# Third matrices and output projections: both halves of the activation in one pass over a whole bank

## The reference, cut to what matters

```
def swiglu(x, w_gate, w_up, w_down):
    return (jax.nn.silu(x @ w_gate) * (x @ w_up)) @ w_down     # w_down: 2816 x 1024

# first model, two layers: x += 0.5*ffn1(norm(x)); x += merged(attention) @ w_out; x += 0.5*ffn2(norm(x))
# second model:
        x = x + g_a * y_l                                      # y_l ends in a product with the output matrix
        x = x + g_m * sq_relu_mlp(modulate(rms_norm_2(x, norm_mlp_g[i]), sh_m, sc_m), mlp_w1[i], mlp_w2[i])
```

## Time and profile before

| | us |
|---|---|
| median of 3 runs | 2549.56 (2544.74 to 2553.31) |
| profiled execution | 2535.18 |
| its span, first to last instruction | 2533.3 |
| TensorE busy in the span | 2472.7 |
| VectorE busy | 1618.0 |
| ScalarE busy | 1191.0 |
| mean granted clock of TensorE | 0.987 |

### The profile page before, as it was taken

The page is one execution under the profiler, slowest core; times in us unless marked ns, Lnnn a source line. Parts: engine busy times, 40 slices in busy tenths (PEclk is TensorE's granted clock), DMA queues, the critical chain, the costliest instruction groups (busy, mean ns, idle before and its releaser), DMA issues.

```text
span 2533.3 us, 42329 instructions
## 1 busy us (share of the span) xinstructions
PE 2472.7 (98%) x18041; PEld 2309.1 (91%) x18041; DVE 1618.0 (64%) x2450; ACT 1191.0 (47%) x1960; POOL 332.4 (13%) x369
## 2 busy tenths in 40 slices
PE   8999999999999899999999999999999999999998
PEld 7999989999999899899999667888888999999998
DVE  4787576778987865767775875542443654556753
ACT  5444566544444355655454553531332534345643
POOL 1321000332022010022331000100001011001000
PEclk9999999999999999999999999999999999999999
DMA  7677544567776756347785120322322433334552
GB/s 252 208 234 211 154 138 134 181 219 241 254 233 216 237 141 196 109 142 251 264 285 165 51 79 17 98 96 89 100 99 85 127 104 113 100 100 152 172 193 100
DMA packets 386385, 401.65 MB, mean 159 GB/s; under 512 B 44695, under 2 KB 370611, under 8 KB 385940
## 3 DMA queue, kind: packets, MB, share of 16 engines
q1 hardware_dynamic: 383448, 391.19, 49.3%
q10 hardware_dynamic: 2748, 7.76, 0.8%
HBM read 394.72 MB, written 4.19 MB: 157 GB/s over the span
## 4 chain that ended last, share of the span: by engine, by line
PE 76%; DVE 15%; ACT 4%; DMA 2%; issue 2%; POOL 1%; ACTq 0%; DVEq 0%; POOLq 0%
PE bank L676 22%; PE bank L677 21%; PE bank L678 21%; DVE rounded L2419 7%; PE bank L684 4%; DVE plain L2404 3%; ACT rounded L1642 2%; DMA plain<-in_ffn_w_down 2%; PE bank L1565 2%; PE bank L689 1%; POOL plain L3497 1%; PE bank L1090 1%; DVE plain L2547 1%; PE bank L1120 1%; PE bank L779 0%
## 5 line engine op out<-in xcount | busy, mean ns | idle before, releaser
L676 PE MATMUL bank<-rounded 128*128 128x256 f32 (+1 forms) x3704 | 1116.6, 301 | 10.0 <-DVE rounded L2419 7.0
L677 PE MATMUL bank<-rounded 128*128 128x256 f32 (+1 forms) x3704 | 1099.4, 297 | 0.0
L678 PE MATMUL bank<-rounded 128*128 128x256 f32 (+1 forms) x3704 | 1099.2, 297 | 0.0
L2419 DVE TENSOR_TENSOR rounded<-plain,rounded 128x1024 fp32r<-128x1024 f32 (+1 forms) x630 | 738.3, 1219 | 459.0 <-ACT rounded L1642 459.0
L1642 ACT ACTIVATE rounded<-plain 128x1024 fp32r<-128x1024 f32 (+1 forms) x630 | 616.0, 1032 | 301.7 <-PE bank L678 186.3
L676 PEld LDWEIGHTS bank<-rounded 128*128 128x128 f32 x3704 | 714.3, 193 | 44.3 <-DVE rounded L2419 9.0
L677 PEld LDWEIGHTS bank<-rounded 128*128 128x128 f32 x3704 | 714.8, 193 | 16.0
L678 PEld LDWEIGHTS bank<-rounded 128*128 128x128 f32 x3704 | 714.2, 193 | 16.4
L676 PE MATMUL bank<-rounded,rounded 128*128 128x256 f32 (+2 forms) x1472 | 452.3, 307 | 17.3 <-DVE plain L2615 10.0
L678 PE MATMUL bank<-rounded,rounded 128*128 128x256 f32 (+2 forms) x1472 | 449.4, 305 | 0.0
L677 PE MATMUL bank<-rounded,rounded 128*128 128x256 f32 (+2 forms) x1472 | 448.7, 305 | 0.0
(11 more groups left out here) (310 smaller groups left out, 1992.2 us busy)
## 6 DMA issues: line engine op xcount, KB each, us to landing
plain<-in_mlp_w SPq DMA_DIRECT2D x64, 1024.0 KB, 5.3
plain<-in_ada_w SPq DMA_DIRECT2D x48, 1024.0 KB, 5.5
plain<-in_ffn_w_gate SPq DMA_DIRECT2D x44, 1024.0 KB, 6.1
plain<-in_ffn_w_up SPq DMA_DIRECT2D x44, 1024.0 KB, 6.0
plain<-in_ffn_w_down SPq DMA_DIRECT2D x32, 1024.0 KB, 5.3
plain<-in_w_in SPq DMA_DIRECT2D x32, 1024.0 KB, 5.4
plain<-in_od_w_in SPq DMA_DIRECT2D x32, 1024.0 KB, 5.7
plain<-in_ffn_w_down SPq DMA_DIRECT2D x16, 768.0 KB, 5.1
```

The costliest lines, as they stand in the source:

```text
L676: pe.matmul(dst, a[0], b[0], start=first and i == 0, stop=False)
L677: pe.matmul(dst, a[0], b[1], start=False, stop=False)
L678: ins = pe.matmul(dst, a[1], b[0], start=False, stop=last and i == n - 1)
L2419: dve.tensor_tensor(low, raw, top, SUB).then_inc(*done(("lo", m, half)))
```

## The change

In 7 of the 8 output groups (o = 0 to 6) of the six kinds of product named above, `apart` takes the place of `product`. It passes the top and the low activations as one moving operand of 512 columns, two pieces of 256 at a distance, under the top weights into the whole bank; then the top activations under the low weights into columns 0 to 255. So columns 0 to 255 hold top by top and low by top, and columns 256 to 511 hold top by low. VectorE adds both parts to the residual, the second one after it has waited for its own first addition. The bank is free and the group done with the second. Group 7 stays as it was. `p0` stays too, since it has 512 columns of tokens, and so does the even mixer.

```
@@ -678,6 +678,20 @@
+    def apart(b, pairs, first=True, last=True):
+
+
+        n = len(pairs)
+        for i, (a, (h, l)) in enumerate(pairs):
+            both = bass.AP(h.tensor, h.offset, [h.ap[0], [l.offset - h.offset, 2], *h.ap[1:]])
+            pe.matmul(b[:, :], a[0], both, start=first and i == 0, stop=False)
+            ins = pe.matmul(b[:, 0:256], a[1], h, start=False, stop=last and i == n - 1)
+        return ins
+
+    def sums(apart_, b):
+
+        return (lambda *a: apart(b, *a)) if apart_ else (lambda *a: product(b[:, 0:256], *a))
@@ -849,8 +863,8 @@
-                    ins = product(bs[j][:, 0:256], [(part(m, k - k0, j * 128), (f.hr[:, k, :], f.lr[:, k, :]))],
-                                  k == 0, k == 21)
+                    ins = sums(2 * blk + j < 7, bs[j])([(part(m, k - k0, j * 128), (f.hr[:, k, :], f.lr[:, k, :]))],
+                                                       k == 0, k == 21)
@@ -2490,6 +2507,20 @@
+    def second(b, o, by, keys):
+
+        for x in new(L.last()):
+            dve.wait_ge(*x)
+        dve.scalar_tensor_tensor(X[:, o, 0:256], b[:, 256:512], by, X[:, o, 0:256], MUL, ADD).then_inc(*done(*keys))
@@ -2612,8 +2643,11 @@
+                    keys = [(s, "x", o), ("free", s, "d", o)]
                     dve.scalar_tensor_tensor(X[:, o, 0:256], M.bank(s, "d", o)[:, 0:256], 0.5, X[:, o, 0:256], MUL,
-                                             ADD).then_inc(*done((s, "x", o), ("free", s, "d", o)))
+                                             ADD).then_inc(*done(*([] if o < 7 else keys)))
+                    if o < 7:
+                        second(M.bank(s, "d", o), o, 0.5, keys)
```

More of the change, by code:

```diff
@@ L1171, in mixer @@
                         keys = [("unit", m)] if j else []
-                        ins = product(bs[j][:, 0:256], [(part(m, k, j * 128), (b_.Mr[:, k, :], b_.Ml[:, k, :]))], k == 0, k == 7)
+                        ins = apart(bs[j], [(part(m, k, j * 128), (b_.Mr[:, k, :], b_.Ml[:, k, :]))], k == 0, k == 7)
                         if k == 7:
@@ L1177, in mixer @@
                     keys = [("unit", m)] if j else []
-                    product(bs[j][:, 0:256], [(part(m, k, j * 128), (b_.Mr[:, k, :], b_.Ml[:, k, :])) for k in range(8)]
+                    sums(2 * blk + j < 7, bs[j])([(part(m, k, j * 128), (b_.Mr[:, k, :], b_.Ml[:, k, :])) for k in range(8)]
                             ).then_inc(*done((s, "wo", 2 * blk + j), *keys))
@@ L1480, in mlp @@
                                 pe.wait_ge(*x)
-                            ins = product(bs[j][:, 0:n], [(part(m, k - k0, j * 128), (b_.hr[:, k, :], b_.lr[:, k, :]))],
-                                          k == 0, k == b_.part - 1)
+                            pairs = [(part(m, k - k0, j * 128), (b_.hr[:, k, :], b_.lr[:, k, :]))]
+                            if l and 2 * blk + j < 7:
+                                ins = apart(bs[j], pairs, k == 0, k == b_.part - 1)
+                            else:
+                                ins = product(bs[j][:, 0:n], pairs, k == 0, k == b_.part - 1)
                         keys = [("unit", m)] if j else []
@@ L1577, in outer @@
                 pe.wait_ge(*x)
-            return product(b[:, 0:256], [(part(m, k % 8, j * 128), (b_.Yr[:, k, :], b_.Yl[:, k, :]))], k == 0, k == 15)
+            return sums(2 * blk + j < 7, b)([(part(m, k % 8, j * 128), (b_.Yr[:, k, :], b_.Yl[:, k, :]))], k == 0, k == 15)
         bs = [[bank(s, "wo", j) for j in range(2)], None, None, None]
@@ L2491, in residual_part, with residual_two @@
                                  MUL, ADD).then_inc(*done((s, "x", o, q), ("free", *name)))
+    def second(b, o, by, keys):
+        for x in new(L.last()):
+            dve.wait_ge(*x)
+        dve.scalar_tensor_tensor(X[:, o, 0:256], b[:, 256:512], by, X[:, o, 0:256], MUL, ADD).then_inc(*done(*keys))
+    def residual_two(s, key, name, o, l, which, *out):
+        for x in new(at(*key)):
+            dve.wait_ge(*x)
+        b, by = M.bank(*name), M.MODS[l][:, 16 + 24 * which + o, 0:1]
+        dve.scalar_tensor_tensor(X[:, o, 0:256], b[:, 0:256], by, X[:, o, 0:256], MUL, ADD).then_inc(*done())
+        second(b, o, by, [out, ("free", *name)])
     def residual(s, key, name, o, l, which, seqs, *out):
@@ L2981, in mixer @@
                     dve.wait_ge(*x)
+                keys = [(s, "x", o), ("free", s, "wo", o)]
                 dve.tensor_tensor(X[:, o, 0:256], M.bank(s, "wo", o)[:, 0:256], X[:, o, 0:256], ADD).then_inc(
-                    *done((s, "x", o), ("free", s, "wo", o)))
+                    *done(*([] if o < 7 else keys)))
+                if o < 7:
+                    second(M.bank(s, "wo", o), o, 1.0, keys)
                 if o:
@@ L3380, in odd @@
                         o = 2 * blk + j
[L3381 removed]
+                        if o < 7:
+                            residual_two(s, (s, "wo", o, 8), (s, "wo", o), o, 1, 0, s, "x", o)
+                        else:
+                            residual(s, (s, "wo", o, 8), (s, "wo", o), o, 1, 0, 1, s, "x", o)
                         b1 = M.mlp[1]
```

6 lines of the change are left out of this document (4 added, 2 removed).

## The result

| | before | after |
|---|---|---|
| median of 13 runs, us | 2547.83 (2541.14 to 2553.31) | 2552.97 (2549.83 to 2569.32) |
| profiled execution, us | 2535.18 | 2553.40 |
| mean granted clock in it | 0.987 | 0.984 |

What follows compares the result with a forecast made beforehand. The prediction took TensorE, with 76% of the chain of waits, as the main bound and VectorE, with 15%, as the bound around the splits. Eight stretch terms summed to +8.9 us: 2549.6 + 8.9 = 2558.5 us, range 2546 to 2570.

Steps and rivals of the forecast that it cites:

- m0: Projection, up to TensorE's wait at 499.39: VectorE's chain holds the path, second additions lengthen its loops; +3.2 us.
- b0: Third matrix, up to TensorE's wait at 700.80: pairs of groups add 0.45, 0.92, 0.68 and 0.92; +2.9 us.
- a0: Third matrix: VectorE's chain up to the last pair +2.0, lower clock after a longer TensorE wait +1.6; +3.6 us.
- a1: Third matrix: VectorE's chain up to the last pair +2.0, low clock's stretch falling into the wait -1.0; +1.0 us.
- b1: Third matrix: TensorE never idle, loads almost as slow; -1.0 us counted of 154 triples' 1.8.
- p1: Last matrix: TensorE never idle, splits ready well ahead, so all 224 triples count; -2.7 us.
- The triple: Two matmuls, one of 512 columns, replace three of 256: 12 ns saved each, 12.8 us for all 1064 (8.8 to 15.9).
- the rival that saves nothing: The 512-column pass costs its columns and a second start, so triples save nothing or little; 2564 us, chance 0.06.
- The second addition: On VectorE, starts 0.45 us after the first; 0.46 us more per group, 26.6 us at most, some 13 on the path.
- Cold starts: Rival: longer stops in first products of b0, a1 and b1 bring the lower clock; 5.5 us more, 2564, chance 0.14.
- Half-absorbed additions: Rival: half of the 12.8 us of lengthening sinks in VectorE's gaps or pace-setting loads; +2.5 us, 2552, gaps' chance 0.20.
- Hidden additions: Rival: VectorE hides the additions, only the triples count; -12.8 us, 2537 (2534 to 2541), chance 0.12.

Runs made afterwards that it cites:

- C1: The change itself, first profile; 2553.40 us in that execution, ratio 1.0034 to the kernel before.
- C2: The change executed once more for its trace, nothing altered; 2562.18 us.
- S: The whole change, with top and low activations side by side in memory, so no jump in the operand; ratio 1.0027 to the kernel before.
- one-piece kernel: The change with the wide matmul's operand as 512 columns in one piece, adding up wrong products; 2547.85 us in its only run.
- V: VectorE's part alone: the kernel before plus 56 second additions of the same columns times zero, each waiting for the first; ratio 1.0057.
- P: TensorE's part alone: the change without its second additions, so top by low is left out; ratio 1.0000 to the kernel before.
- N: V with each second instruction not waiting for the first, writing to the bank's unused half; ratio 1.0027 to the kernel before.

## Why the prediction came out right, step by step

Own share means: the average of C1, C2, S and the one-piece kernel less the average of the profiles that are the kernel before in that stretch. In `o` and `p1` it is C1 and C2 alone, since the other two have no jump, and in `m0` and `m1` a profile with a low clock is left out and named.

| stretch | forecast | own share | |
|---|---|---|---|
| `m0` | +3.2 | +2.84 (3.1 with S's low clock) | mechanism right, one link too many |
| `m1` | +2.7 | +2.57; 4.13 with a low clock | right |
| `b0` | +2.9 | +2.7 | right, but unchanged programs spread over 2.8 |
| `a0` | +3.6 | +1.3 | chain 1.7 for 2.0, clock wrong |
| `a1` | +1.0 | +1.3 | right by two errors |
| `b1` | -1.0 | +0.3 | wrong; unchanged programs spread over 0.6 |
| `o` | -0.8 | -0.3 | triple mis-sized |
| `p1` | -2.7 | -1.3 | triple mis-sized |
| sum | +8.9 | +9.4 to +10 | measured +8.7 (4.6 to 13), 5.1 by the medians |

One part of the change's cost falls behind these stretches and stands in no row. The first 28 us of `m0` and of `m1` are each 0.3 us longer in the change (C1, C2, S and one piece), and the first 7 us of `e` 0.2. V has 0.3 and 0.15 there, P nothing, and each repeats within 0.02 us; in the table above they lie in the rows of the attentions and of `e`, where a low clock's 1.5 to 8 us hide them. The 0.3 is what the forecast had for group 7's addition and weighting in `a0` and `a1`, and it is right; for the 0.2 behind `b1` it had nothing. With these 0.8 us the sum is +10.2 to +10.8, still inside the interval.

**The triple** is the term that was mis-sized: 12 ns taken, 5.6 to 5.9 measured, below the lower end of the range (8.3). It came from `p0`'s contiguous 512 columns. The prediction named the jump as unknown, gave it no price above the tile's, and so cut its own range too short; the jump's 4 ns is what it lacked, and the rest is that the wide step without a jump is 234 and not 230, less 2 ns that the narrow step gives back (118.6 for 120.8). The prediction's last sentence named this sign, a step "well off 230 ns", and 238 is that. In `p1` it is the whole miss. For the triples alone the truth lay between the forecast and the rival that saves nothing.

**The second addition** was right to the hundredth (0.45 us behind the first, 0.92 a loop), and so was its place. In `m0` the four pairs of groups came out at 0.54, 0.92, 0.92 and 0.45; the forecast had 0.53, 0.92, 0.92 and 0.92. Group 7 has no second addition, and its weighting is only as late as group 6's makes it. The forecast counted a link that isn't there: its term for the last pair fails by 0.47, less the 0.1 it took off.

**The stop for a weighting** in `b0`'s first product was to be 2.7 us. It is 2.08 in C2, 0.63 in C1, where a low clock at 471 us had held TensorE back, but the end of the stretch is the same in both. The 2.5 us forecast in `b1` were 2.07. In `a1` none of note came: TensorE waits there 1.25 us for a split.

**`a0` and `a1`.** The chain up to the last pair has an own share of 1.7 us in both, near the forecast 2.0. The clock's +1.6 in `a0` rested on one execution in which the clock had stayed up; the kernel before pays this too, and the own share of the last pair is -0.4, in `a1` as well (forecast -1.0). The sum was saved by errors of opposite sign: `a0` was 2.3 too high (2.0 with the 0.3 us behind it), and `b1`, `o` and `p1` together were 3.2 too low. That the forecast came within 0.2 us of the measurement is luck; that `m0`, `m1` and `b0` carry most of it is not.

**`b0`.** The size came out (the forecast's four terms add up to 2.97, of which it took 2.9), but not by the steps that the forecast summed. In C1 TensorE stops before the last pair of groups for a split, and the low clock follows:

```profile
676.10 0.79 PE L687 MATMUL bank<-rounded,rounded 128*128 128x512 f32 x1 [2.22 <-DVE rounded L2436]
...
676.00:679.00 3.00, 2.90 (x9) 2.51 (x10) 2.97 (x5) 0.71 (x1) 0.00 (x0) 0.50 1.00 367
```

A stop of this size and a low clock behind it stand there in all four profiles with the whole of the change, and in none of the ten without it, P and V included; V and N have the additions, and +2.5 and +2.6, without it. So here there is a cold start that comes with both halves together: an early TensorE and a late VectorE. What it adds at the end of the stretch (0.9 us between V and the change) is within what the loads move there, and stays open.

**`b1`.** The forecast let seven second additions cost nothing, for want of weightings behind them, and gave the triples 1.0. V and N, with the additions alone, gave +0.6 and +0.8, but one unchanged program gave +0.6 too, so what the additions cost there is not clear of the spread. In the first trace of before the closest split of `b1`'s third matrix is ready 0.17 us ahead of its use, and TensorE never stops. In V it stops 0.36 us for that split, in C1 0.77 us, and 0.69 us for another:

```profile
1330.06 0.51 PE L687 MATMUL bank<-rounded,rounded 128*128 128x512 f32 x1 [0.77 <-DVE rounded L2436]
...
1347.94 0.50 PE L687 MATMUL bank<-rounded,rounded 128*128 128x512 f32 x1 [0.69 <-DVE rounded L2436]
```

An unchanged program stops 0.36 us for that split as well. So the margin of 0.17 us is what the forecast's "0.2 to 1.5 us ahead" had and didn't price, and how much of the loss is the additions' and how much the loads' stays open.

**The rivals.** Cold starts came in part, and not all where the forecast put them: in `b0`'s third matrix, ahead of its last pair of groups, in all four profiles, behind the stop in `m1` in one of four, in `m0` at the price of 0.9 us in one. Half-absorbed additions (+2.5) are below the interval. Hidden additions are out by V. That a triple saves nothing is out by its measured 5.6 ns, and that rival's +14.5 lies above the interval.

## What to carry to other kernels

To move work from the engine with the most busy time to the one with the second most is a gain only in stretches where the first one's next start hangs on its own last instruction; here these were two of eight, and restricting the change to them and laying the operand out without its jump turned +8.7 us into a gain of 2.4 by the traces. The layout gave two thirds more in `p1`. And before a low clock, or the lack of one, enters a sum, look whether a second profile of the same program shows it: a term that rests on one execution's clock is a draw, not a price.

## What was not expected of the hardware

- A moving operand of 2 x 256 columns at a distance takes 238.1 ns a step, the same in one piece 234.1; but in `o` it is 236 to 237 either way.
- The wait of a VectorE instruction for its own predecessor costs 0.11 us in this pair of instructions, measured by taking away what makes it wait (0.34 us from start to start for 0.45).
- The same stop of 3.19 us in the same program is followed by 2.4 GHz once and by 1.2 GHz six times; stops of 2.07 and 2.08 us are followed by 1.2 and by 2.4.
- Where neither clock nor loads play a part, stretches of 35 to 90 us repeat to 0.02 us from one execution to the next, so that effects of 0.3 us can be read from a profile when the time of the whole varies by 10 to 20.
